# First loads of a streaming-encoder kernel: x and weights all issued by SyncE, in the order in which they are used

## The reference

```
x <- LN(ALPHA*x + 0.5*SwiGLU_1(x))                      # w13: 1024 x 5632, w2: 2816 x 1024
x <- LN(ALPHA*x + W_out [pool_group(x) || mla_group(x)])
x <- LN(ALPHA*x + CrossAttn(x, mem))
x <- LN(ALPHA*x + 0.5*SwiGLU_2(x))
swiglu(x, w13, w2):  gate, up = split(x @ w13);  (silu(gate) * up) @ w2
```

## Time and profile before

| | |
|---|---|
| time, median of 3 runs | 1083.3 us (1083.29 to 1083.43) |
| the profiled execution | 1084.16 us, span of its trace 1082.4 us |
| PE busy | 1071.2 us, 99% |
| DVE busy | 869.5 us, 80% |
| ACT busy | 530.2 us, 49% |
| DMA | 203.96 MB, mean 188 GB/s |

### The profile page before, as it was taken

One profiled execution on the slowest core, in us unless ns is written; L12 is line 12 of the kernel. 1 busy time (PEld: TensorE's weight loads), 2 busy tenths in 40 slices (PEclk: granted clock), 3 DMA queues, 4 the chain that ended last, 5 costly groups with the idle time before them and its releaser, 6 DMA issues.

```text
span 1082.4 us, 16425 instructions
## 1 busy us (share of the span) xinstructions
PE 1071.2 (99%) x5558; PEld 921.8 (85%) x5558; DVE 869.5 (80%) x1520; ACT 530.2 (49%) x731; POOL 84.6 (8%) x141
## 2 busy tenths in 40 slices
PE   8999999999999999999999999999999999999997
PEld 7888888999998888888888888889999988888885
DVE  6988777897855898878688887878988668987885
ACT  6544443656544644444455444445565545444442
POOL 0015001220000000000000000001300000000000
PEclk9999999999999999999999999999999999999999
DMA  9876675455564486666567666654455654866641
GB/s 321 285 225 191 208 229 154 133 155 190 170 223 150 139 257 211 192 204 189 159 182 247 204 191 194 197 157 134 154 174 163 222 166 137 266 190 203 185 144 39
DMA packets 156466, 203.96 MB, mean 188 GB/s; under 512 B 12960, under 2 KB 136096, under 8 KB 156416
## 3 DMA queue, kind: packets, MB, share of 16 engines
q1 hardware_dynamic: 152112, 192.55, 56.6%
q0 software_dynamic: 3488, 9.97, 3.4%
q10 hardware_dynamic: 816, 0.79, 0.2%
HBM read 202.22 MB, written 1.05 MB: 188 GB/s over the span
## 4 chain that ended last, share of the span: by engine, by line
PE 97%; DVE 2%; DMA 1%; issue 0%; POOL 0%; ACT 0%; DVEq 0%; POOLq 0%; ACTq 0%
PE ps L620 94%; PE ps L703 1%; DMA raw<-in_ffn_w 1%; DVE w_lo L1468 0%; PE ps L1108 0%; PE ps L874 0%; DVE xT L1481 0%; PE ps L961 0%; PE ps L1014 0%; DVE tmp L1716 0%; DVE x L1623 0%; PE ps L1069 0%; DVE tmp L1715 0%; DVE x L1599 0%; PE ps L1071 0%
## 5 line engine op out<-in xcount | busy, mean ns | idle before, releaser
L1468 DVE TENSOR_TENSOR w_lo<-raw,w_hi 128x1024 fp32r<-128x1024 f32 (+3 forms) x246 | 297.2, 1220 | 47.0 <-ACT w_hi L1202 44.8
L1202 ACT CAST w_hi<-raw 128x1024 fp32r<-128x1024 f32 (+3 forms) x246 | 252.8, 1044 | 161.7 <-PE ps L620 150.9
L620 PE MATMUL ps<-w_hi,xT 128*128 128x512 f32 (+1 forms) x912 | 286.9, 389 | 1.8 <-ACT w_hi L1194 1.8
L620 PEld LDWEIGHTS ps<-w_hi,xT 128*128 128x128 f32 x912 | 170.9, 188 | 37.8 <-issue 3.3
L1537 DVE STREAM_TRANSPOSE hidden_T<-ev 32x128 f32<-32x128 f32 x624 | 189.0, 303 | 11.2
L620 PE MATMUL ps<-w_hi,mixT 128*128 128x512 f32 x688 | 197.6, 390 | 0.0
L620 PE MATMUL ps<-v_flat,xT 128*128 128x512 f32 (+1 forms) x660 | 177.0, 389 | 0.0
L620 PE MATMUL ps<-w_lo,xT 128*128 128x512 f32 (+1 forms) x456 | 175.2, 388 | 0.0
L1202 ACT CAST v_flat<-raw 128x1024 fp32r<-128x1024 f32 (+1 forms) x114 | 118.2, 1045 | 85.2 <-PE ps L620 83.5
L620 PEld LDWEIGHTS ps<-w_hi,mixT 128*128 128x128 f32 x688 | 128.6, 188 | 26.3
L620 PEld LDWEIGHTS ps<-v_flat,xT 128*128 128x128 f32 x660 | 123.8, 188 | 25.4 <-DVE cqp L1468 0.2
(11 more groups left out here) (188 smaller groups left out, 1251.9 us busy)
## 6 DMA issues: line engine op xcount, KB each, us to landing
raw<-in_ffn_w SPq DMA_DIRECT2D x350, 256.0 KB, 3.5
raw<-in_ffn_w SPq DMA_DIRECT2D x88, 512.0 KB, 4.1
raw<-in_mem_wkv SPq DMA_DIRECT2D x32, 512.0 KB, 4.4
raw<-in_w_out SPq DMA_DIRECT2D x16, 512.0 KB, 5.1
raw<-in_mem_wq SPq DMA_DIRECT2D x16, 512.0 KB, 4.5
raw<-in_mem_wo SPq DMA_DIRECT2D x16, 512.0 KB, 6.4
gb<-in_ln_g POOLq DMA_DIRECT2D x16, 256.0 KB, 5.4
gb<-in_ln_b POOLq DMA_DIRECT2D x16, 256.0 KB, 4.8
```

The source lines that it names most:

```text
L620: return nc.tensor.matmul(dst, stand, move, start=start, stop=stop, skip_group_check=True)
L1202: nc.scalar.copy(slot_hi[slot[n]][:, 0:size], raw[:, n % RAW, 0:size]).then_inc(hi_done, 1)
L1468: nc.vector.tensor_tensor(slot_lo[slot[n]][:, s], raw[:, n % RAW, s], slot_hi[slot[n]][:, s].bitcast(F32), ALU.subtract).then_inc(lo_done, 1)
```

## The change

All transfers at the start are issued by SP, ACT issues none. The first piece of x is cut into two pieces of one block each (128 KB), so there are five pieces of x with five semaphores. SP's order becomes: x block 0, first half of unit 0, x block 1, second half of unit 0, x blocks 2 and 3, both halves of unit 1, x blocks 4 and 5, unit 2, x blocks 6 and 7, unit 3, and from there as before. ACT and DVE round and split x block 1 between the two halves of unit 0, and PE's waits on x follow the new count of pieces.

```
-        x_columns_landed = [sem(f"x_columns_landed{j}") for j in range(KT // 2)]
+        x_columns_landed = [sem(f"x_columns_landed{j}") for j in range(5)]
...
+        X_PIECES = [slice(0, 1), slice(1, 2), slice(2, 4), slice(4, 6), slice(6, 8)]
...
-            part = a["x_columns"].rearrange("(k p) s -> p k s", p=P)[:, 2 * j:2 * j + 2, :]
-            queue.dma_start(x_columns[:, 2 * j:2 * j + 2, :], part).then_inc(x_columns_landed[j], 16)
+            part = a["x_columns"].rearrange("(k p) s -> p k s", p=P)[:, X_PIECES[j], :]
+            queue.dma_start(x_columns[:, X_PIECES[j], :], part).then_inc(x_columns_landed[j], 16)
...
# SP
+                        if n < 4:
+                            load_x_columns(sp, n + (n > 0))
                         if n < 2:
-                            load_half(sp, n, n)
+                            load_half(sp, n, 0)
+                            if n == 0:
+                                load_x_columns(sp, 1)
+                            load_half(sp, n, 1)
                         else:
                             load(n, source[n][1])
-                        if n < 3:
-                            load_x_columns(sp, n + 1)
...
# PE, up_first
-                            pe.wait_ge(x_hi, j + 1)
+                            arrived = 1 if j == 0 and columns == [0] else j + 2
+                            pe.wait_ge(x_hi, arrived)
...
-                            pe.wait_ge(x_lo, j + 1)
+                            pe.wait_ge(x_lo, arrived)
...
# ACT
-            load_x_columns(act, 0)
-            load_half(act, 0, 1)
-            load_half(act, 1, 0)
             act.wait_ge(dve_step, 1)
             ready_gate(ev[:, 0, 0:1])
             for j in range(4):
-                round_x(j)
+                round_x(j + (j > 0))
                 if j < 2:
-                    for t in range(2):
-                        half_hi(j, t)
+                    half_hi(j, 0)
+                    if j == 0:
+                        round_x(1)
+                    half_hi(j, 1)
                 else:
                     ahead_to(j + 1)
...
# DVE: the same order, with split_x and half_lo
```

More of the change, by code:

```diff
@@ L1415, in round_x @@
             def round_x(j):
-                part = slice(2 * j, 2 * j + 2)
+                part = X_PIECES[j]
                 act.wait_ge(x_columns_landed[j], 16)
                 nc.scalar.copy(xT[:, part, 0, :], x_columns[:, part, :]).then_inc(x_hi, 1)
-            load_x_columns(act, 0)
-            load_half(act, 0, 1)
-            load_half(act, 1, 0)
             act.wait_ge(dve_step, 1)
@@ L1864, in _ @@
             for j in range(4):
-                split_x(j)
+                split_x(j + (j > 0))
                 if j < 2:
-                    for t in range(2):
-                        half_lo(j, t)
+                    half_lo(j, 0)
+                    if j == 0:
+                        split_x(1)
+                    half_lo(j, 1)
                 else:
```

## The result

The changed kernel takes 1084.91 us (median of 22 runs, 1084.45 to 1085.72) against 1083.42 us before (median of 22 runs, 1082.88 to 1084.15): 1.49 us more, ratio 1.0013 with a 95% interval of 1.0007 to 1.0018. The forecast was 1082.4 us, 0.9 us less, with a range of 1081.3 to 1083.8. The change is clear of noise, and goes the other way.

The account below looks back on a forecast made before the run. PE, 99% busy, was taken to bound the kernel, its start limited by unit 2's landing at 9.8 + 0.8 = 10.6 us; PE starting it at 11.8 instead of 12.70 gave 1083.3 - 0.9 = 1082.4 us, range 1081.3 to 1083.8.

Parts of the forecast that it names:

- What binds: Whole kernel: PE is busy 99% of the span, so only its start and few idle places can be won.
- the hole before the second group: PE's idle time between its first two groups of six products: expected to shrink from 1.47 us to under 0.5.
- a new wait of 0.5 us: Before unit 2: PE would newly wait about 0.5 us for ACT's rounding, a sign to look for in the profile.
- The place after it, unit 7: Next close place after unit 2: 0.7 us of cover; mem should come 0.9 us sooner, otherwise the gain is capped.
- The sum for unit 2: Arrival of unit 2: 2.8 + 6.7 + 0.3 = 9.8 us, plus a 0.8 us tail, so landing at 10.6.
- the 2.8 us of the forecast: Start of the DMA stream from SP's queue: 2.8 us, with bounds 2.1 and 2.85.
- I add 0.3 us because the first four transfers (768 KB) need four issues: Start of the stream: 0.3 us added for issuing the first four transfers, until about 3.2 us, and for half-size ones.
- The window of 3.75 to 7 us: Early DMA stream: one queue would show over 300 GB/s and a share near 1.
- The tail: Lag from mean arrival of unit 2's last byte to its landing: taken at 0.8 us, bounds 0.35 and 2.1.
- the 79% share: Engines 79% busy at 244 GB/s in 3.75 to 5.25 us before: guessed to mean two queues cause the unevenness.
- A difference at the start carries over one for one, so I take it from the median: End of the kernel: the 0.9 us gain at unit 2 is subtracted from the median, 1083.3 - 0.9 = 1082.4 us.
- A: Rival: the tail stays, unit 2 lands at 11.9 us, 0.4 later, time 1083.7 (1083.0 with an earlier stream); chance 0.25.
- B: Rival: one queue cannot feed the engines at the start, unit 2 lands at 12.9 us, time 1084.7; chance 0.06.

Follow-up runs that it names:

- second trace of before: The unchanged kernel profiled again, no edit: this execution took 1083.57 us, with unit 2 rounded at 10.86 us.
- third trace of before: The unchanged kernel profiled a third time, no edit: this execution took 1084.14 us, with unit 2 rounded at 11.50 us.
- two-issuer version: Kernel before, with x in its four old pieces, the first two issued by ScalarE, and SyncE issuing weights and remaining x in order of use: 1082.85 us.
- one-issuer version: Kernel before, with all first loads issued by SyncE in order of use and x in its four old pieces: 1083.93 us.
- early empty issue: One unneeded 1 KB transfer added right after x's first piece, to the kernel with all first loads on SyncE and x in four pieces: 1084.62 us.

## Why the prediction was wrong

**What binds, right.** The change can only touch the start, the hole before the second group shrinks (1.47 to 0.99 us in the waits, though to under 0.5 was forecast, since the second half of unit 0 was there at 7.0 us and not at 6.1), and unit 2 takes over as the bound with a new wait of 0.5 us for L1208, which is the size that was forecast. The place after it, unit 7, cost nothing: mem's rounding moved by 0.40 us with unit 2 (21.96 against 21.56). Because unit 2 decides, mending the order ahead of it gained nothing.

**The sum for unit 2, wrong in two terms.** The stream started earlier than the 2.8 us of the forecast, and than its bound of 2.1 (188 GB/s in 1.88 to 2.5 us): x's first piece came from SyncE's queue as early as it had from ScalarE's, and 2.8 was the time of the weights alone. The rate of 353 GB/s once the queue is full was right (358). But the step "I add 0.3 us because the first four transfers (768 KB) need four issues" was far too small: 252 GB/s up to 8.5 us are 1.67 MB, and the rest of the 2.36 MB takes 1.9 us at 358 GB/s, so the bytes of unit 2 were through at 10.4 us, not 9.8. From 2.1 us at full rate they would have been at 8.8: the thin start cost 1.6 us where the sum had 0.3. The kernel before had 0.6 of these (9.4 us), so the change added 1.0. The window of 3.75 to 7 us, for which over 300 GB/s and a share near 1 were forecast, shows 234 and 0.84, which is one of the forecast's own signs of being wrong. The traces place the loss, behind the two half-size pieces; the runs show that x whole (0.5 us by the medians instead of 1.5) and two issuers in the right order lose less, and that an issue of 1 KB at the head costs 0.7 us by the medians. That the time of SyncE's issues, 0.40 to 0.66 us each and one behind the other, is what thins the stream fits the first stretch. For the second it is not shown, since two issued transfers were waiting there.

**The tail, also mis-sized.** Taken at 0.8 us. By 11.88 us the stream had moved 1.67 + 1.21 = 2.88 MB, 0.52 MB or 1.5 us past unit 2's last byte. In the second trace of before it is 302 GB/s to 8.5 and 362 after, 2.85 MB by 10.86, so 1.4 us; in the first it is 2.1. The tail varies by 0.7 us from run to run of the same kernel. With one queue it is 1.0 to 1.7 us in seven traces, mostly shorter than before, but with two issuers and the right order it is as short (0.9 and 1.2), so it does not follow the number of queues. Reading the 79% share as a sign that two queues disturb each other was the mistake: the third trace of before has a share of 0.99 at 315 GB/s in that stretch and the same tail of 2.1 us, and the changed kernel with its one queue has 0.68 at 163 GB/s. What makes the tail stays open.

```profile
3.75:5.25 1.50, 1.22 (x9) 1.05 (x8) 0.22 (x2) 0.88 (x2) 0.00 (x0) 1.00 0.68 163
```

Together the two terms, less the 0.7 us by which the start was taken too late, put unit 2 at 11.9 instead of 10.6 us.

**The baseline.** "A difference at the start carries over one for one, so I take it from the median" holds for the difference of two typical starts. The trace of before was not typical: its execution took 1084.16, its median is 1083.42. 11.49 us for unit 2 belonged to a late run, so there was 0.7 us less to win than the sum took for granted. Of the 2.5 us between forecast and result, 1.3 are unit 2 (PE at 13.08 instead of 11.8), 0.86 are this subtraction, 0.27 are what the first two traces' executions differ by beyond PE's lag, and 0.1 is the changed kernel's trace being below its median.

**The rivals.** A named the landing of unit 2 exactly (11.9 us, PE 0.4 us later) but gave 1083.7 for it, for the same fault of baseline. That it hit was luck: it was made of a stream through at 9.8 and a tail of 2.1 us, and 10.4 and 1.5 were measured. B, "One queue cannot feed the engines at the start", came nearest to what happened, a thinner stream at the start. Its point of decision was set wrongly: in 3.75 to 7 us the queue moved 0.76 MB, just above the 0.7 that I had named, and the kernel was slower all the same, because the stream had been thin before 3.25 us too. Its 1084.7 is near the result by luck as well: it had unit 2 landing at 12.9 instead of 11.9 us, which the fault of baseline made up for; it had 6 chances in 100. On the Trainium skill's sentence from "DMA: Bandwidth & Descriptors", section "Issuing engines are not separate DMA queues": several issuers "will only save the time on the sequencer it takes to initiate the DMA". The runs agree with that as far as they go: the two-issuer version is 1.1 us faster than the one-issuer version with the same pieces in nearly the same order (1082.85 and 1083.93, all 11 runs of the one below all 11 of the other, though in two sets). That it is issue time that is saved they do not show.

## What to carry to other kernels

At the start of this kernel the right order gained nothing while the stream itself got thinner: two issuing engines in the order of use gave the fastest version (1082.85 us), one issuer with half-size first pieces the slowest (1084.9). So try to spread the first few large transfers over two issuing engines, and do not cut the first pieces smaller without looking at the stream behind them. Look for the next place where the stream binds before counting a hole as won. And before a trace is used as the baseline of a small difference, compare its own execution's time with the median: a start that varies by 0.7 us from run to run is as large as the effect.

## What the runs showed of the hardware

- A transfer of 1 KB costs SyncE 0.45 to 0.60 us of issue, a transfer of 128 KB 0.40 to 0.58 us, one of 256 KB about 0.6 (0.46 as the first of a queue). The size hardly enters.
- Full queue: 350 to 368 GB/s in 8.5 to 12 us, whoever issued (325 only with the early empty issue). First 6.6 us: 246 to 331 GB/s, depending on who issued what.
- The same kernel's traces differ in when unit 2's last byte lands by 0.64 us (10.86 and 11.50) at almost the same mean rate (302 and 311 GB/s). In all three traces all but one of its parts are there by 10.60 to 10.72 us; the last part decides.
- Behind a first transfer of 128 KB the stream is thin for most of a microsecond (74 to 156 GB/s in 2.5 to 3.25 us, six traces), behind one of 256 KB it is not (285 to 378, seven traces).
- The third issuer, GpSimd, did not help although its transfer was the same size: the weights that SyncE had issued landed later. Its packets go through a queue of their own and start 2.3 us after its issue began, against 1.1 us for ScalarE's transfer in the same trace; whether that is the cause is not shown.
